# Sums of squares for the row norms: one float32 product replaced by two products of high and low parts in five of eight passes

## The reference, cut to what matters

```python
def rms_norm(t, g):
    tf = t.astype(jnp.float32)
    y = tf * lax.rsqrt(jnp.mean(tf * tf, axis=-1, keepdims=True) + NORM_EPS)
    return (y * g.astype(jnp.float32)).astype(t.dtype)
...
        dq = rms_norm(dq.reshape(B, S, DIFF_HEADS, 2, HEAD_DIM), diff_q_norm_g[i])
        dk = rms_norm(dk.reshape(B, S, DIFF_HEADS, 2, HEAD_DIM), diff_k_norm_g[i])
...
        bq = rms_norm(bq.reshape(B, S, DIL_HEADS, HEAD_DIM), dil_q_norm_g[i])
        bk = rms_norm(bk.reshape(B, S, DIL_HEADS, HEAD_DIM), dil_k_norm_g[i])
```

## Time and profile before

| | |
|---|---|
| median of 3 runs | 2904.7 us (2899.4 to 2905.01) |
| profiled execution, its own time | 2902.29 us |
| its span | 2900.5 us |
| mean granted clock of TensorE | 0.985 of full speed |
| PE, DVE, ACT, POOL busy | 95%, 59%, 36%, 32% of the span |
| `mixers_phase` | about 1893 to 2730 us of the span |

### The profile page before, as it was taken

How to read it: one execution, slowest core, us unless ns; L and a number is a source line. 1 busy time by engine, 2 the same in 40 slices (tenths; PEclk the granted TensorE clock), 3 DMA queues, 4 the chain that set the end, 5 groups by cost and what they waited for, 6 DMA issues and landing times. The chain is left out here.

```text
span 2900.5 us, 39452 instructions
## 1 busy us (share of the span) xinstructions
PE 2757.6 (95%) x15534; PEld 2112.9 (73%) x15534; DVE 1714.0 (59%) x2674; ACT 1047.3 (36%) x1735; POOL 935.8 (32%) x549
## 2 busy tenths in 40 slices
PE   6999999999999899999999999979999999998999
PEld 5979797977878677777776887755666666666777
DVE  5787878785021344444455114766676677777586
ACT  4342524343010233233333002345666654444232
POOL 2232323232664122122122334542222143432465
PEclk9999999999999899999999999999999999999999
DMA  4241423233533111110112324421101111113544
GB/s 166 56 88 66 87 73 80 74 81 137 183 109 102 38 52 46 51 48 30 52 45 106 109 73 165 156 93 43 40 19 43 41 44 37 37 44 102 183 149 112
DMA packets 113751, 236.53 MB, mean 82 GB/s; under 512 B 9120, under 2 KB 52896, under 8 KB 113568
## 3 DMA queue, kind: packets, MB, share of 16 engines
q1 hardware_dynamic: 63312, 172.14, 18.2%
q10 hardware_dynamic: 50256, 61.87, 7.3%
HBM read 189.88 MB, written 44.11 MB: 81 GB/s over the span
## 5 line engine op out<-in xcount | busy, mean ns | idle before, releaser
L79 PE MATMUL psum<-u_h,w_hi 128*128 128x512 f32 (+2 forms) x2624 | 1011.1, 385 | 23.8 <-DVE u_h L2874 6.0
L80 PE MATMUL psum<-u_h,w_hi 128*128 128x512 f32 (+2 forms) x2624 | 967.6, 369 | 0.0
L81 PE MATMUL psum<-u_h,w_lo 128*128 128x512 f32 (+2 forms) x2624 | 966.5, 368 | 0.0
L135 POOL TENSOR_SCALAR w_hi<-w_raw 128x1024 fp32r<-128x1024 f32 x212 | 240.7, 1135 | 1469.0 <-ACTq L1324 518.6
L79 PEld LDWEIGHTS psum<-u_h,w_hi 128*128 128x128 f32 x2624 | 497.3, 190 | 155.4 <-issue 68.3
L137 POOL TENSOR_TENSOR w_lo<-w_raw,w_hi 128x1024 fp32r<-128x1024 f32 x212 | 545.9, 2575 | 17.7
L81 PEld LDWEIGHTS psum<-u_h,w_lo 128*128 128x128 f32 x2624 | 497.1, 189 | 71.5
L80 PEld LDWEIGHTS psum<-u_h,w_hi 128*128 128x128 f32 x2624 | 497.6, 190 | 69.5 <-issue 8.9
L2544 ACT ACTIVATE a_exp<-a_exp 128x1024 f32<-128x1024 f32 x96 | 101.6, 1059 | 154.9 <-DVE a_exp L2703 77.6
L1349 ACT ACTIVATE f_exp<-psum 128x1024 f32<-128x1024 f32 (+4 forms) x112 | 82.1, 734 | 192.9 <-PE psum L1207 94.0
L1445 DVE CUSTOM_DVE_ANT_0 f_junk<-psum,f_decay,f_max 128x512 f32<-128x512 f32 (+2 forms) x96 | 60.3, 666 | 133.9 <-PE psum L1230 120.6
(11 more groups left out here) (431 smaller groups left out, 4425.1 us busy)
## 6 DMA issues: line engine op xcount, KB each, us to landing
w_raw<-in_w_all SPq DMA_DIRECT2D x212, 512.0 KB, 3.5
sums_rows<-s_acs ACTq DMA_DIRECT2D x32, 512.0 KB, 8.7
f_decay<-s_nc SPq DMA_DIRECT2D x16, 520.0 KB, 5.6
s_y<-conv_out ACTq DMA_DIRECT2D x16, 512.0 KB, 3.0
yo_raw<-s_y ACTq DMA_DIRECT2D x8, 1024.0 KB, 9.3
x_tok<-in_x SPq DMA_DIRECT2D x8, 512.0 KB, 8.0
s_xT<-xT SPq DMA_DIRECT2D x8, 512.0 KB, 4.9
s_pssd<-fox_last ACTq DMA_DIRECT2D x16, 256.0 KB, 2.2
```

Of the source, the lines that this page charges most:

```text
L79: nc.tensor.matmul(out, w_hi[:, k], a_hi, start=(k == 0 and first), stop=False)
L80: nc.tensor.matmul(out, w_hi[:, k], a_lo, start=False, stop=False)
L81: return nc.tensor.matmul(out, w_lo[:, k], a_hi, start=False, stop=(k == kk - 1 and final))
L135: self.nc.gpsimd.tensor_scalar(self.hi[:, r], self.raw[:, r], 1.0, 1.0, ALU.mult, ALU.mult).then_inc(self.hi_done, 1)
```

## The change

Three parts. In passes q = 0 to 4 (`halved`), the sum of squares is no longer one product of the float32 squares with the float32 matrix of ones, but two accumulated products of float32r numbers: with a high part of the squares and with the low part that is left. The matrix of ones is copied once to float32r (`exact`, in free columns behind the activations). The two parts are made by POOL in halves of `tok`: a copy of `sq` that rounds, and a subtraction (`squares_low`). POOL does this in the slot in which the group ends, ahead of the row splits and weight splits of that slot. PE waits for the low part (`low_ok`) where it waited for the square. Third, for q = 1 to 4 the items of `GQ0` and `GQ1` become late ones, on PE and on ACT.

```diff
+    halved = lambda q: q <= DIFF
...
-    is_late = lambda p, x, it: it[0] == "E" and x == 6 or it[0] in ("D", "P", "EB", "EP") or it[0] == "T" and (p < 0 or x == 13)
+    is_late = lambda p, x, it: it[0] == "S" and 0 < it[1] <= DIFF and it[2] in (GQ0, GQ1) or it[0] == "E" and x == 6 or it[0] in ("D", "P", "EB", "EP") or it[0] == "T" and (p < 0 or x == 13)
...
+            def squares_low(q, g):
+
+                c = number_of(q, g)
+                high, low = (tok[:, i, 512 * (c % 2):512 * (c % 2) + 512] for i in range(2))
+                pool.wait_ge(sq_ok, c + 1)
+                nc.gpsimd.tensor_copy(high, sq[:, c % 2]).then_inc(low_ok, 1)
+                pool.wait_ge(low_ok, 2 * c + 1)
+                nc.gpsimd.tensor_tensor(low, sq[:, c % 2], high.bitcast(F32), ALU.subtract).then_inc(low_ok, 1)
...
             for p in range(-1, PASSES):
                 q = p + 1
                 for x in range(U):
+                    for g, k in share(q, x) if q < PASSES and halved(q) else []:
+                        if k == KT - 1 and g <= GQ1:
+                            squares_low(q, g)
                     if q < PASSES and x in normed_at(q):
                         split_rows(q, normed_at(q)[x])
...
                 if kind == "S":
-                    pe.wait_ge(sq_ok, number_of(q, g) + 1)
-                    last = nc.tensor.matmul(bank, K.pairs[:, :], sq[:, number_of(q, g) % 2], start=True, stop=True)
+                    c = number_of(q, g)
+                    if halved(q):
+                        pe.wait_ge(const_ok, 1)
+                        pe.wait_ge(low_ok, 2 * c + 2)
+                        for i in range(2):
+                            last = nc.tensor.matmul(bank, exact, tok[:, i, 512 * (c % 2):512 * (c % 2) + 512], start=(i == 0), stop=(i == 1))
+                    else:
+                        pe.wait_ge(sq_ok, c + 1)
+                        last = nc.tensor.matmul(bank, K.pairs[:, :], sq[:, c % 2], start=True, stop=True)
...
             dve.wait_ge(cleared, 1)
+            nc.vector.tensor_copy(exact, K.pairs[:, :])
```

More of the change, by code:

```diff
@@ L1901, in _, with mixers_phase @@
             split(KT - 1)
-def mixers_phase(nc, K, u_hi, u_lo, strips, pt, S, V_p, acc0, o1, x1, row_of):
+def mixers_phase(nc, K, u_hi, u_lo, exact, strips, pt, S, V_p, acc0, o1, x1, row_of):
     PASSES, DIFF, U, SPAN = 8, 4, 16, 2 * T - P
@@ L2026, in mixers_phase @@
         stored = [s(f"stored{i}") for i in range(4)]
-        tok_ok = s("tokens")
+        tok_ok, low_ok = s("tokens"), s("squares_low")
         rootx, invx, scalex, addx_ok, sqx_ok, sumx = (s(n) for n in ["rootx", "invx", "scalex", "addx", "sqx", "sumx"])
@@ L3203, in program @@
                 W.base = W.base + 2 * KT
-                mixers_phase(nc, K, h_hi, h_lo, strips, pt, S, V_p, acc0, o1, x1, mix_row)
+                mixers_phase(nc, K, h_hi, h_lo, uh[:, 2 * KT * T:2 * KT * T + P], strips, pt, S, V_p, acc0, o1, x1, mix_row)
                 clear_semaphores(nc)
```

## The result

The median of four runs is 2936.9 us (2935.2 to 2939.3) against 2902.7 us of before: ratio 1.0114, 95% interval 1.0102 to 1.0127. So the kernel became 34 us slower; 2933 was predicted, in a range of 2911 to 2950.

A forecast was written before the change was run, and what follows sets the result against it. PE was taken to bound the kernel. Opening 13.4, three passes 11.1 and q = 4 4.6 us made 29.1 on the profiled 2902.3, 2931.4; with half the median's 2.4 us excess, 2933, range 2911 to 2950.

The forecast's parts named there:

- What bounds it: PE, busy 95% of 2900.5 us and full in the passes: time off it shortens the kernel, its waits lengthen it.
- The opening: In q = 0, POOL's waits for squares ahead of tile and row splits make the first keys 13.4 us late (9 to 18).
- K1's wait: Slot 4 of a pass: PE waits 1.8 us for K1's parts, and Q0's square comes 0.9 us later.
- ACT's wait at Q0: ACT's copy of Q0 to `un` needs K0's row split, now behind Q0's parts on POOL, and starts 4.3 us later.
- Q1's sum in slot 7: PE waits there for Q1's parts, ready at 2140.4; slot 8 starts at 2144.4 to 2145.2 instead of 2141.10.
- The passes' term: Halved passes after the opening: 3.7 us each, 11.1 us for three, plus 4.6 us for q = 4 with longer row splits.
- the clock as a rival of its own: PE's waits drop stretches of passes and opening to half rate: 2943 to 2948 us; chance 0.13, shared with contention.
- the 3 to 5 us that I gave as a sign: Sign that the forecast holds: passes longer by 3 to 5 us each.
- The rule against it: Two-input SBUF DVE instructions and SBUF-reading POOL ones exclude each other: up to 10 us over four passes, 2943; counted at nothing.
- What the change could win: PE time saved by products and late sums: some 2.1 us a pass, 8.5 us over q = 1 to 4, opening nothing.

The follow-up runs named there:

- Experiments 2: Changed kernel with parts and two products only in the opening (q = 0), no sum late: 2918.9 us, ratio 1.0056 to the kernel before.
- experiment 8: Changed kernel with the opening's weight splits of slots 1 and 4 put before POOL's waits for squares: 2929.1 us, ratio 1.0093 to the kernel before.
- experiment 3: As experiment 1, but in slot 4 POOL makes Q0's parts after K0's row split: 2914.4 us, ratio 1.0042 to the kernel before.
- experiment 1: Changed kernel with the opening (q = 0) kept on the float32 product, no parts there: 2923.4 us, ratio 1.0072 to the kernel before.
- experiment 4: As experiment 3, with K1's sum late too, on PE and ACT: 2904.7 us, ratio 1.0009 to the kernel before.
- experiment 10: As experiment 4, but PE multiplies the float32 squares; parts are made unused, ACT alone waits for them: 2908.5 us, ratio 1.0022 to the kernel before.
- experiment 9: Kernel before with K1, Q0, Q1 sums late and parts and two products for K0 and K1 alone, q = 1 to 4: 2894.3 us, ratio 0.9970.
- experiment 5: As experiment 4, with slot 4's weight split ahead of K0's row split and Q0's parts, q = 1 to 4: 2907.9 us, ratio 1.0021 to the kernel before.
- experiment 6: As experiment 5, but PE makes one float32 product and the parts go unused: 2909.7 us, ratio 1.0026 to the kernel before.
- experiment 7: Kernel before, float32 products and no parts, only the sums of K1, Q0 and Q1 late in q = 1 to 4: 2897.4 us, ratio 0.9984.

## Why the prediction was right, point by point

- *What bounds it.* Right. PE's idle time is the loss, and the distance never shrinks after a halved pass.
- *The opening.* 13.4 us predicted, 13.3 measured. Step by step: V0 at 1914.4 (1915.12), K1's square ending at 1948.4 (1949.2), Q1's tile until 1954.1 (1954.65), the copy of K1 behind K0's row split at 1956.1 (1956.77), first keys at 1969.5 (1969.73). Experiments 2 and 8 confirm the place: alone it costs 16 us in the median and 13.5 in the trace, and moving two weight splits takes 7 off. That experiment 8 left 6 us, more than expected, shows what the order of parts and row splits carries. The steps came out one by one, so this hit is no luck.
- *K1's wait.* Right while the clock stays up: 1.8 us predicted, 1.67 measured, and Q0's square 0.9 us late, net of what K0 and K1 win, where q = 1 and 2 show 1.1 (from K0's square to Q0's). In q = 3 and 4 it is 2.2: the matmuls after the wait run at the lower clock, 0.63 us each at 2241.92, and the stretch up to Q0's square has a granted clock of 0.83.
- *ACT's wait at Q0.* Right: 4.1 us of POOL work after the square, 3.99 us of idle time in q = 3 (4.33 in q = 1 and 2, 4.91 in q = 4); putting the row split first brought it to 0.79 and the kernel 9 us down (experiment 3).
- *Q1's sum in slot 7.* The wrong step. I had PE wait there for the parts. It waits earlier, 1.58 us ahead of slot 7's scores, for the rows that ACT copies after `exps`; by the time it reaches Q1's sum the parts are there in q = 2 and 3, and it waits only 0.61 and 0.44 us in q = 1 and 4. The sum of the chain came out nearly the same, because Q1's square and that copy stand next to each other on ACT; that this term still fitted is partly luck.
- *The passes' term.* 15.7 us predicted, 21.0 measured (4.2, 4.8, 5.6, 6.4). A pass at a granted clock of 1.00 grew by 4.2 us (q = 1) or 4.1 (q = 2 of experiment 1) where I took 3.7: the walk is short by 0.5 us a pass. The rest is the clock: 1.00 in q = 1, as it was in all passes before, but 0.98, 0.97 and 0.97 in the next three. Experiment 1 has the same passes with the clock lost later, which prices it: q = 2 grew by 4.1 us at 1.00 and by 4.8 at 0.98, q = 3 by 4.9 at 0.98 and 5.6 at 0.97. I had the clock as a rival of its own, at 0.13, with 1.7 us a pass; it came on top of the forecast instead of in its place. So 2936.9 lies near 2933 because the opening was right, and the passes' 5 us too little were within the range. Two passes are longer than the 3 to 5 us that I gave as a sign.
- *The rule against it.* I gave contention no share in the sum, and for the changed kernel that holds: there DVE waits for ACT while the weight split runs (DVE's first `lse_rows` operation takes 0.17 us at 2254.89). It is the next obstacle: once ACT's wait is removed, PE stands idle for 1.5 us a pass behind it (experiments 3, 4, 10), and it costs 2.1 us a pass (experiment 10).
- *What the change could win.* 8.5 us was a sum of prices, and no order tried reached it. 0.4 us for K0 and for K1 are real (experiment 9), as predicted. For Q0 and Q1 the traces disagree. At equal clock, q = 2 of experiment 5 is 1.2 us shorter than that of experiment 6, but q = 2 of experiment 4 only 0.6 us shorter than that of experiment 10, less than K0 and K1 give alone. The late place, which the forecast did not price apart from the products, gives 4.3 us without any parts (experiment 7).

Left open: when the clock falls after a wait and when it does not (the last section has the waits), and whether parts for Q0 and Q1 could be placed so that neither ACT, DVE nor the weight split notices; two orders besides that of the changed kernel were tried, and neither does it.

## What to carry to other kernels

Before moving work to an engine that is two thirds idle, read its queue: a wait that is put in front of ready work delays that work by the whole wait, and here the work behind it (a weight tile, a row split) was what PE and ACT needed next. Try the change in order alone first; here it gave half of the best result, and the products themselves paid only where their parts were ready well ahead, in a gap of POOL that nobody stood behind. And when one wait is removed, look at what the shifted work now overlaps.

## What the runs showed that I had not expected

A DVE operation on 128x8 numbers with two inputs in SBUF took 2.31 us instead of 0.17 when POOL's subtraction on 128x1024 had started 0.1 us before it (experiments 4 and 10): the price is that of the other engine's instruction, not its own, so a tiny operation is as exposed as a large one.

And the clock did not follow the length of a wait. In the kernel before, PE waits 2.14 us in q = 4, and the granted clock of that pass is 1.00:

```profile
2358.19 0.50 PE L2305 MATMUL psum<-a_khi,a_qhi 64*128 64x256 f32 x4 [2.14 <-DVE a_maxrows L2762]
```

In the changed kernel it ran at the 1.2 GHz level for about 3.4 us after a wait of 1.67 us in q = 3 (0.43 us from matmul to matmul from 2241.5 to 2242.8) and again after one of 1.58 us; with waits of the same length q = 1 kept a mean of 1.00. In experiment 10, where 1.58 us is the only wait of PE's over 0.3 us in the first half of a pass, it fell after it in two passes of four. In these runs, where the clock fell after a wait of 1.6 to 2.4 us, the pass was 0.7 to 1.4 us longer for it, and one execution doesn't show whether it will fall in the next.
